# Moving the small attention matmuls inside the gate projections of a hybrid attention and expert block

## The chip, the cores and the metric

The kernel runs on one core of a Trainium2 chip. The time is the device time of one execution in microseconds (us). The engines are named as in the profile: PE is TensorE (matmul), PEld its weight loads, DVE is VectorE, ACT is ScalarE, POOL is GpSimd, SP is SyncE, which here only issues transfers. "L917" is line 917 of the kernel. A row-half is one of the two groups of 64 rows of the array: operands in partitions 0 to 63 use one, those in 64 to 127 the other.

## The reference

256 tokens of width 1024, all in f32, one layer. Shortened:

```python
h = rms_norm(x, norm1_g)
q, k, v, qi, ki, wi, pool_in, gate_a, gate_p = split(h @ w_in)
#    512 128 128 256 64  4   512      1024    1024 columns
q, k = rope(rms_norm(q)), rope(rms_norm(k))        # 8 query heads, 2 key heads of 64
qi, ki = partial_rope(qi), partial_rope(layer_norm(ki))
score = sum_over_heads(relu(qi @ ki.T) * wi)       # 4 index heads
sel = top_k(where(admissible, score, -inf), 64)    # per query
attn = softmax(q @ k[sel].T * scale) @ v[sel]
pooled = per_group_linear(trailing_mean(pool_in) - pool_in) * pool_scale
merged = sigmoid(gate_a) * (attn @ w_a) + sigmoid(gate_p) * (pooled @ w_b)
x = x + merged @ w_out
h2 = rms_norm(x, norm2_g)
x = x + moe(h2)   # router, best 4 of 32 experts, gate_up 1024 x 2048, clamped SwiGLU, down 1024 x 1024
```

## The kernel before

The 256 tokens are two row blocks b of 128. The normalised input is held transposed as hT. The projection with w_in is cut into eight groups of columns (`groups`, L208): 512 with K, V and QI, 68 with KI and the index weights, 512 of Q, 512 of pooling input, then two of 512 for each gate. `projection(j)` (L907) computes group j for both row blocks: two halves of the contraction, each one unit of weights, two row blocks and four steps k of 128 rows, so 16 products, each of which appears as two MATMUL records. Its results lie in one of three pairs of PSUM banks. ScalarE takes them out (`job` L394, `gate_job` L401).

All small matmuls (transposes, scores, mixing) write one of two further banks, `TB[j % 2]`, in a fixed order of numbered jobs TJ_... (L229). `t_job(j)` (L881) waits until job j - 2 has been read; each job is read by one named engine in program order (`tcopy` on ScalarE L408 and on VectorE L668, score readers L654, the pooling L678).

TensorE's program is written out by hand and runs in its order. Before the change it reads: projections 0 to 3; the turns of K, QI and KI and the index scores (L969 to L985, four jobs L0 and L1); projection 4; the turns of Q; projection 5; the attention scores (L993 to L1004, S0 for block 0 and S1 for block 1); projection 6; the turns of the probabilities; projection 7; the mixing with the pooling bands (L1021 to L1023), the attention output (L1032), the per-group map (L1041); the two branch products with w_a, then those with w_b (`branch`, L929, one call per row block); the turn of merged block 0 (L1059); then the product with w_out (L1103 on, with the second turn and the router inside it) and the experts.

VectorE prepares K, KI, QI and Q (L584 to L621), does the top 64 selection (L623 to L643, eight rounds of MAX8 and MATCH_REPLACE8 for each row block), masks the scores while reading them out of the banks (L654), finds the maxima, and scales the probabilities (L665, L666). ScalarE does Exp (L439). Later VectorE multiplies the gates in (`gated`, L683) and adds the branches (L697).

SP issues the weight transfers in one queue. The 24 units of the first part (`pre_unit`, L257) go into twelve half slots. Ten slots of 2 MB then serve the experts: eight for gate and up weights (`gu_slot`, L85), two for down weights. Several hold attention data first, so that each has its own condition for its first load (L282 to L298): slot 0 after projection 6, slot 1 after projection 7, slots 6 and 7 after the attention output, slots 2 and 8 after the branch with w_a, slots 3 and 9 after that with w_b, slots 4 and 5 after w_out. From then on a slot is refilled when its expert is done with it, in the order of `gates_a`, `gates_b`, `downs_a`, `downs_b`. The experts go in 16 pairs with 64 tokens each.

Of the kernel before, what the change touches and what calls it, by code (L numbers as in the profile page):

```python
# [5 lines left out]
P = 128  # L6
# [56 lines left out]
def block_kernel(nc, x_d, pos_d, w_in, w_a, w_b, w_out, mix_d, router_d, w_gu, w_dn, b_dn,  # L63
# [6 lines left out]
    with ctx:  # L70
# [17 lines left out]
        kvqi_t, q_t, pool_t, kqT_t = (slot[6][:, 1024 * j:1024 * j + 1024] for j in range(4))  # L88
        ptb, rt_t = slot[7][:, 0:3072], slot[7][:, 3072:4096]
        qT_t, attnT_t = slot[8][:, 0:1024], slot[8][:, 1024:2048]  # L90
        kdup_t, kidup_t, kiT_t = slot[8][:, 2048:2560], slot[8][:, 2560:2816], slot[8][:, 2816:3072]
        mixw_t, work_t = slot[8][:, 3072:3584], slot[8][:, 3584:4096]
        rel, pooledT_t = slot[9][:, 0:1024], slot[9][:, 1024:2048]
        bands_t, kiwi_t = slot[9][:, 2048:3584], slot[9][:, 3584:3720]
# [31 lines left out]
        kvqi, kiwi = v3(kvqi_t[:, :], NB), v3(kiwi_t[:, :], NB)  # L126
# [14 lines left out]
        mixedT, pooledT = v3(rel, GROUPS), v3(pooledT_t, GROUPS)  # L141
# [82 lines left out]
        def dn_src(e, j):  # L224
# [15 lines left out]
        LAST_OF_BRANCH = {17: 2 * (BJ_WA + NB), 19: 2 * (BJ_WB + NB), 23: 2 * (BJ_WO + NB)}  # L240
# [4 lines left out]
        def _(sp):  # L245
# [44 lines left out]
            sp.wait_ge(job_ready, 2 * (BJ_WA + NB))  # L290
# [3 lines left out]
            sp.wait_ge(job_ready, 2 * (BJ_WB + NB))  # L294
# [78 lines left out]
        def _(act):  # L373
# [43 lines left out]
            job(0, kvqi)  # L417
            job(1, kiwi)
# [28 lines left out]
            for j in range(2):  # L447
                tcopy(TJ_MIX + j, mixedT[:, 2 * j:2 * j + 2, :])
# [60 lines left out]
        def _(dve):  # L509
# [162 lines left out]
            tcopy(TJ_P0 + 1, PT[0][:, 0, 4:8, :])  # L672
            tcopy(TJ_P1 + 1, PT[1][:, 0, 4:8, :])
            tcopy(TJ_P1 + 3, PT[1][:, 1, 4:8, :])

            for j in range(2):
# [3 lines left out]
                                ALU.mult).then_inc(t_read[(TJ_POOL + j) % 2], 1)  # L680
            dve.wait_ge(job_read, 16)
# [193 lines left out]
        def _(pe):  # L875
# [31 lines left out]
            def projection(j, between=None):  # L907
# [61 lines left out]
            pe.wait_ge(roped, 1)  # L969
            transposes(TJ_K, [kdup[:, b, kv, :] for b in range(NB) for kv in range(KV)])  # L970
            pe.wait_ge(roped, 3)
            transposes(TJ_QI, [kvqi[:, b, 256 + P * g:256 + P * g + P] for b in range(NB) for g in range(2)])
            transposes(TJ_KI, [kidup[:, b, :] for b in range(NB)])

            short_read(pe, TJ_KI + 1)
            for b in range(NB):
                nk = P * (b + 1)
                for par in range(2):
                    dst = t_job((TJ_L0, TJ_L1)[b] + par)
                    for i in range(2):  # L980
                        h = 2 * i + par
                        r = 64 * (h % 2)
                        ins = MM(dst[:, i * nk:i * nk + nk], qiT[r:r + 64, h // 2, b * P:b * P + P], kiT_t[r:r + 64, 0:nk],
                                 start=True, stop=True)
                    ins.then_inc(t_ready, 1)  # L985
            projection(4)
            pe.wait_ge(roped, 4)
            for b in range(NB):
                transposes(TJ_Q + b, [qq[:, b, P * g:P * g + P] for g in range(4)])
            projection(5)  # L990

            short_read(pe, TJ_Q + 2)
            for b in range(NB):  # L993
                nk = P * (b + 1)
                per = BANK // nk
                for g in range(HEADS // per):
                    dst = t_job((TJ_S0 if b == 0 else TJ_S1) + g)
                    h0 = 4 * (g // 2) + g % 2 if b == 1 else g
                    for i in range(per):
                        h = h0 + 2 * i  # L1000
                        r = 64 * (h % 2)
                        ins = MM(dst[:, i * nk:i * nk + nk], qT[r:r + 64, h // 2, b * P:b * P + P], kT[r:r + 64, h // 4, 0:nk],
# [336 lines left out]
```

## Time and profile before

| | us |
|---|---|
| median of three timed runs | 1127.81 (1127.17 to 1128.42) |
| profiled execution | 1124.1 |
| its span, first to last instruction | 1122.3 |
| PE busy | 1051.0 (94%) |
| DVE busy | 290.4 (26%) |
| ACT busy | 118.0 (11%) |
| transfers, mean | 383 GB/s over the span |

The page divides the span into 40 slices of 28 us; the GB/s row is what the transfer engines moved in each. A busy PE is not PE at its peak: matmuls overlap, and the distance from one start to the next is the cost. The profiled execution is one run; its time is 3.7 us below the median of the timed ones.

### The profile page before, as it was taken

To read this page: it belongs to the slowest core of one execution; us is meant where nothing else is said; L and a number is where in the kernel's file an instruction comes from. 1 tells how busy PE (TensorE), PEld (TensorE's weight loads), DVE (VectorE), ACT (ScalarE), POOL (GpSimd) and SP (SyncE) were. 2 spreads that over 40 slices of the span, in tenths; PEclk is the share of its full clock that TensorE was granted. 3 is DMA by queue.
4 is the path that set the end of the run, shared out by engine and by line. 5 is a ranking of instruction groups with operands and counts; after the bars stand their busy time and mean duration, and the time that the engine had idled before them with its cause. 6 is when DMAs were issued, how large, how long until landed. Compare 5 with 4: busy or idle time off the path is not lost.

```text
span 1122.3 us, 11997 instructions
## 1 busy us (share of the span) xinstructions
PE 1051.0 (94%) x4830; PEld 439.1 (39%) x4830; DVE 290.4 (26%) x592; ACT 118.0 (11%) x210; POOL 7.7 (1%) x16
## 2 busy tenths in 40 slices
PE   7999999999999999999999989898989899999988
PEld 4444545543434343434343424242424243333332
DVE  2654032332222222221212121221212212212221
ACT  3124101201000000000000000000000000000001
POOL 2000000000000000000000000000000000000000
PEclk9999999999999999999999999999999999999999
DMA  9932573899999999999999999999999999999995
GB/s 335 392 130 84 216 279 117 336 385 430 428 427 428 429 425 427 422 429 429 428 428 427 430 429 429 429 428 429 427 430 429 429 428 428 430 426 430 429 429 220
DMA packets 40256, 430.32 MB, mean 383 GB/s; under 512 B 5024, under 2 KB 5152, under 8 KB 15536
## 3 DMA queue, kind: packets, MB, share of 16 engines
q1 hardware_dynamic: 39280, 428.11, 91.4%
q0 software_dynamic: 672, 1.91, 0.5%
q8 instruction: 11, 0.18, 0.1%
q10 hardware_dynamic: 288, 0.08, 0.0%
q14 instruction: 5, 0.04, 0.0%
HBM read 429.03 MB, written 1.05 MB: 383 GB/s over the span
## 4 chain that ended last, share of the span: by engine, by line
PE 73%; DMA 22%; DVE 2%; issue 1%; ACT 0%; SPq 0%; DVEq 0%
PE bank L1194 28%; DMA slot<-w_gate_up_dram 18%; PE bank L1219 14%; PE bank L917 9%; PE bank L1139 5%; PE bank L1168 5%; DMA slot<-w_down_dram 4%; PE bank L941 4%; PE bank L1208 2%; DVE x L838 2%; PE bank L1117 1%; PE bank L892 1%; PE bank L1179 1%; DMA consts<-consts_dram 0%; PE bank L1235 0%
## 5 line engine op out<-in xcount | busy, mean ns | idle before, releaser
L1194 PE MATMUL bank<-slot,scr 128*64 128x512 f32 x2048 | 458.8, 596 | 20.5 <-DMA slot<-w_gate_up_dram 20.4
L1194 PEld LDWEIGHTS bank<-slot,scr 128*64 128x64 f32 x2048 | 142.3, 137 | 305.9 <-issue 268.6
L1219 PE MATMUL bank<-slot,scr 128*64 128x512 f32 x1008 | 229.1, 596 | 11.1 <-DMA slot<-w_down_dram 10.4
L813 DVE COPY scr<-bank 128x512 f32<-128x512 f32 x32 | 22.1, 691 | 456.6 <-PE bank L1194 456.6
L1219 PEld LDWEIGHTS bank<-slot,scr 128*64 128x64 f32 x1008 | 68.6, 137 | 144.9 <-issue 120.0
L917 PE MATMUL bank<-slot,scr 128*128 128x512 f32 (+1 forms) x256 | 103.3, 563 | 0.8 <-DVE scr L531 0.8
L1168 PE MATMUL bank<-scr 64*128 64x512 f32 x240 | 59.6, 613 | 22.0 <-DVE x L838 22.0
L838 DVE TENSOR_TENSOR x<-bank,x 128x512 f32<-128x512 f32 x64 | 41.4, 686 | 105.3 <-PE bank L1168 103.1
L819 DVE TENSOR_TENSOR scr<-bank,bgu 128x512 f32<-128x512 f32 x64 | 41.2, 686 | 104.9 <-PE bank L1208 104.9
L917 PEld LDWEIGHTS bank<-slot,scr 128*128 128x128 f32 x256 | 46.5, 194 | 53.7 <-issue 52.5
L1139 PEld LDWEIGHTS bank<-scr,xn 128*128 128x128 f32 x480 | 57.7, 196 | 12.2 <-issue 12.2
L1139 PE MATMUL bank<-scr,xn 128*128 128x128 f32 x480 | 60.5, 285 | 0.0
L473 ACT ACTIVATE scr<-bank 128x512 f32<-128x512 f32 x32 | 19.1, 597 | 383.7 <-PE bank L1194 383.7
L1168 PEld LDWEIGHTS bank<-scr 64*128 64x128 f32 x240 | 22.0, 186 | 59.4 <-DVE x L838 34.0
L1208 PEld LDWEIGHTS bank<-consts,scr 128*128 128x128 f32 x256 | 33.3, 210 | 26.9 <-issue 26.9
L1208 PE MATMUL bank<-consts,scr 128*128 128x128 f32 x256 | 39.3, 296 | 0.9 <-ACT scr L473 0.9
L477 ACT ACTIVATE scr<-scr 128x512 f32<-128x512 f32 x32 | 20.2, 631 | 183.2 <-DVE scr L823 183.2
L485 ACT ACTIVATE scr<-bank 128x512 f32<-128x512 f32 x16 | 9.6, 597 | 208.2 <-PE bank L1179 208.2
L941 PE MATMUL bank<-slot 128*128 128x512 f32 x64 | 27.6, 592 | 0.0
L481 ACT ACTIVATE scr<-bank 128x512 f32<-128x512 f32 x31 | 18.5, 597 | 45.4 <-PE bank L1219 45.4
L827 DVE SCALAR_TENSOR_TENSOR scr<-scr 128x512 f32<-128x512 f32 x32 | 22.2, 693 | 3.3
L831 DVE TENSOR_TENSOR scr<-scr 128x512 f32<-128x512 f32 x32 | 22.2, 692 | 1.1
(184 smaller groups left out, 389.1 us busy)
## 6 DMA issues: line engine op xcount, KB each, us to landing
slot<-w_gate_up_dram SPq DMA_DIRECT2D x128, 2048.0 KB, 29.2
slot<-w_down_dram SPq DMA_DIRECT2D x63, 2048.0 KB, 20.9
slot<-w_in_dram SPq DMA_DIRECT2D x14, 1024.0 KB, 15.5
slot<-w_out_dram SPq DMA_DIRECT2D x4, 1024.0 KB, 4.9
slot<-w_branch_attn_dram SPq DMA_DIRECT2D x2, 1024.0 KB, 13.9
slot<-w_branch_pool_dram SPq DMA_DIRECT2D x2, 1024.0 KB, 8.5
slot<-w_down_dram SPq DMA_DIRECT2D x2, 1024.0 KB, 7.2
x<-x_dram SPq DMA_DIRECT2D x2, 512.0 KB, 5.7
```

What stands on the lines that cost most here:

```text
L813: V.tensor_copy(gu_sb[:, 512:1024], GB[1][:, :]).then_inc(gu_copied[1], 1)
L819: V.tensor_tensor(gu1[:, 4 * h:4 * h + 4, :, :], v4(TU[h][:, :], 4, 2), bias.unsqueeze(3).to_broadcast([P, 4, 2, T]), ALU.add).then_inc(re ...
L827: V.scalar_tensor_tensor(out=up1, in0=up1, scalar=1.0, in1=gu1[:, :, 0, :], op0=ALU.add, op1=ALU.mult).then_inc(prod_ready, 1)
L831: V.tensor_tensor(actT[e], up1, sg, ALU.mult).then_inc(act_ready, 1)
L838: V.tensor_tensor(x[:, b, 512 * h:512 * h + 512], XY[h][:, :], x[:, b, 512 * h:512 * h + 512], ALU.add).then_inc(read[f"Y{j}"], 1)
L917: ins = MM(bank[PAIR_BANKS[j % 3][b]][:, 0:n], hT[:, kc, b * P:b * P + P], w[:, k, :], start=kc == 0, stop=kc == KC - 1)
L941: ins = MM(bank[PAIR_BANKS[j % 3][h]][:, :], lhs[:, k, b * P:b * P + P], w[:, k % 2, 512 * h:512 * h + 512], start=k == 0, stop=k == nk - 1)
L1139: ins = MM(XY[h][:, k * P:k * P + P], xn[:, b, c0:c0 + 2 * P - 1:2], selb[:, b * P:b * P + P], start=b == 0, stop=b == NB - 1)
L1168: ins = MM(XY[h][:, :], selgT[T * h:T * h + T, SEQ * e + b * P:SEQ * e + b * P + P], dsb[T * h:T * h + T, 512 * e:512 * e + 512], start=e ...
L1194: ins = MM(GB[h][T * g:T * g + T, :], xgT[:, k, T * e:T * e + T], gu_slot[s][:, c0:c0 + 512], start=k == 0, stop=k == KC - 1)
L1208: ins = nc.tensor.transpose(TU[h][:, k * P:k * P + P], gu_sb[:, c0:c0 + 4 * P - 3:4], ident)
L1219: ins = MM(DB[T * h:T * h + T, :], actT[e][:, c, :], v3(dn_slot[j][:, :], 4)[:, k, 512 * h:512 * h + 512], start=c == 0, stop=c == KC - 1)
```

## The change

- **Narrow columns.** The groups of 512 (K, V, QI) and 68 (KI, weights) become two groups of 290 columns in one tile kvx.
- **Inside the projections.** `projection` takes a table `under`: at step 8 * half + 4 * b + k it calls the functions named there ahead of the product. Turns of K, QI, KI and the index scores go into projection 4; the turns of Q and the scores of row block 0 into 5; the scores of block 1 and the mixing into 6; the turns of the probabilities and the per-group map into 7; the attention output into the first branch product; the turn of merged block 0 into the last.
- **Alternating halves.** In the index scores and the attention scores two jobs are opened together, and successive products use row-half 0 and 1 in turn, into the two banks. Before, a job's products all used one half.
- **Pooling branch first.** The w_b branch comes before the w_a branch, in TensorE's, VectorE's and SP's order; w_b is loaded first. VectorE's second turn copy of a block comes straight after its sum.
- **Orders.** The jobs are renumbered. ScalarE's two mix copies come between the two blocks of Exp. VectorE reads the pooling results between the probability copies.
- **Slots.** The attention tiles are laid out anew in slots 6, 8 and 9, and slots 8 and 9 change places in `gu_slot`.

The core of the diff; the tile layout and the functions that only wrap old code (turn_k, turn_qi, turn_ki, index_scores, turn_probs, mix, pooled, attended, take_pooled) are left out. index_scores has the loop order of scores.

```diff
-        gu_slot = [slot[s] for s in (0, 1, 6, 7, 2, 8, 3, 9)]
+        gu_slot = [slot[s] for s in (0, 1, 6, 7, 2, 9, 3, 8)]
...
-        groups = [(C_K, 512), (C_KI, 68), (C_Q, 512), (C_POOL, 512),
+        groups = [(C_K, 290), (C_K + 290, 290), (C_Q, 512), (C_POOL, 512),
                   (C_GA, 512), (C_GA + 512, 512), (C_GP, 512), (C_GP + 512, 512)]
...
-            w, r0 = [(w_a, 16), (w_b, 18), (w_out, 20)][0 if u < 18 else 1 if u < 20 else 2]
+            w, r0 = [(w_b, 16), (w_a, 18), (w_out, 20)][0 if u < 18 else 1 if u < 20 else 2]
...
-            0, 4, 5, 6, 7, 9, 11, 25, 29, 13, 15, 19, 21, 27, 31, ((35, 36), (38, 40)), (37, 41), (39, 42))
-
-        BJ_WA, BJ_WB, BJ_WO = 8, 10, 12
+            0, 4, 5, 6, 7, 9, 11, 19, 23, 13, 15, 21, 25, 29, 31, ((35, 36), (38, 40)), (37, 41), (39, 42))
+
...
-            sp.wait_ge(job_ready, 2 * (BJ_WA + NB))
+            sp.wait_ge(job_ready, 2 * (BJ_WB + NB))
...
-            sp.wait_ge(job_ready, 2 * (BJ_WB + NB))
+            sp.wait_ge(job_ready, 2 * (BJ_WA + NB))
...
-            job(0, kvqi)
-            job(1, kiwi)
+            job(0, kvx[:, :, 0:290])
+            job(1, kvx[:, :, 290:580])
...
+                if b == 0:
+                    for j in range(2):
+                        tcopy(TJ_MIX + j, mixedT[:, 2 * j:2 * j + 2, :])
...
-            for j in range(2):
-                tcopy(TJ_MIX + j, mixedT[:, 2 * j:2 * j + 2, :])
...
+            tcopy(TJ_P0 + 1, PT[0][:, 0, 4:8, :])
+            for j in range(2):
+                take_pooled(j)
+            tcopy(TJ_P1 + 1, PT[1][:, 0, 4:8, :])
+            tcopy(TJ_P1 + 3, PT[1][:, 1, 4:8, :])
...
+                gated(BJ_WB, b, sigp)
+            for b in range(NB):
                 gated(BJ_WA, b, siga)
-
-            for b in range(NB):
-                gated(BJ_WB, b, sigp)
-                dve.wait_ge(job_read, 2 * (BJ_WB + b) + 2)
+                dve.wait_ge(job_read, 2 * (BJ_WA + b) + 2)
                 V.tensor_tensor(siga[:, b, :], siga[:, b, :], sigp[:, b, :], ALU.add).then_inc(merged_ready, 1)
-            for j in (1, 3):
-                tcopy(TJ_M + j, hT[:, 4:8, (j // 2) * P:(j // 2) * P + P])
+                tcopy(TJ_M + 2 * b + 1, hT[:, 4:8, b * P:b * P + P])
...
+            def projection(j, between=None, under={}):
...
+                            for call in under.get(8 * half + 4 * b + k, ()):
+                                call()
...
+            def turn_q(b):
+                pe.wait_ge(roped, 4)
...
+            def scores(b, pair):
+                short_read(pe, TJ_Q + 2)
                 nk = P * (b + 1)
                 per = BANK // nk
+                j = (TJ_S0, TJ_S1)[b] + 2 * pair
+                dst = [t_job(j + par) for par in range(2)]
+                for i in range(per):
+                    for par in range(2):
+                        h = 4 * pair + par + 2 * i
+                        r = 64 * par
+                        ins = MM(dst[par][:, i * nk:i * nk + nk], qT[r:r + 64, h // 2, b * P:b * P + P], kT[r:r + 64, h // 4, 0:nk],
                                  start=True, stop=True)
+                        if i == per - 1:
+                            ins.then_inc(t_ready, 1)
...
+            projection(4, under={2: [turn_k], 4: [turn_qi], 6: [turn_ki], 9: [lambda: index_scores(0)],
+                                 12: [lambda: index_scores(1)]})
+            projection(5, under={4: [lambda: turn_q(0)], 6: [lambda: turn_q(1)], 13: [lambda: scores(0, 0)]})
+            projection(6, under={1: [lambda: scores(1, 0)], 4: [lambda: scores(1, 1)], 6: [lambda: mix(0)],
+                                 8: [lambda: mix(1)]})
+            projection(7, under={1: [lambda: turn_probs(0, 0, 0)], 3: [lambda: turn_probs(0, 0, 1)],
+                                 5: [lambda: pooled(0)], 7: [lambda: pooled(1)],
+                                 9: [lambda: turn_probs(1, 0, 0)], 11: [lambda: turn_probs(1, 0, 1)],
+                                 13: [lambda: turn_probs(1, 1, 0)], 15: [lambda: turn_probs(1, 1, 1)]})
             short_read(pe, TJ_POOL + 2)
-            for b in range(NB):
-                branch(b, BJ_WB, 18, 4, pooledT)
+            branch(0, BJ_WB, 16, 4, pooledT, ((2, lambda: attended(0)), (3, lambda: attended(1))))
+            branch(1, BJ_WB, 16, 4, pooledT)
+            short_read(pe, TJ_O + 2)
+            branch(0, BJ_WA, 18, 4, attnT)
...
-            turn_merged(0)
+            branch(1, BJ_WA, 18, 4, attnT, ((2, lambda: turn_merged(0)),))
```

## Rows read from the trace of the kernel before

**Rows 1.** The page's part 2, 40 slices of the span, DMA share and GB/s.
```profile
DMA  9932573899999999999999999999999999999995
GB/s 335 392 130 84 216 279 117 336 385 430 428 427 428 429 425 427 422 429 429 428 428 427 430 429 429 429 428 429 427 430 429 429 428 428 430 426 430 429 429 220
```

**Rows 2.** The chain that ended last, in order of time: start us, us, what.
```profile
1067.52 26.57 DMA slot<-w_down_dram
```

**Rows 3.** Waits: engine, line, waited for: us in total, times, longest.
```profile
SPq L255 <- PE bank L1117: 30.1, 1, 30.1
...
DVE slot L654 <- PE bank L1002: 14.5, 1, 14.5
```

**Rows 4.** Timeline of SP: start us, us, what; x8 counts merged issues.
```profile
209.71 37.51 SPq L266 DMA_DIRECT2D slot<-w_gate_up_dram  x8
```

**Rows 5.** Timeline of TensorE, 55 to 213 us, columns as above, idle time before in brackets.
```profile
55.29 1.04 PE L892 MATMUL bank<-consts,slot 128*128 128x128 f32 x8
...
61.09 14.65 PE L917 MATMUL bank<-slot,scr 128*128 128x512 f32 x32
...
76.46 13.90 PE L917 MATMUL bank<-slot,scr 128*128 128x512 f32 x32
90.29 1.71 PE L1002 MATMUL bank<-slot 64*128 64x128 f32 x16
...
94.96 1.73 PE L1002 MATMUL bank<-slot 64*128 64x256 f32 x8 [0.93 <-DVE xn L654]
96.61 14.00 PE L917 MATMUL bank<-slot,scr 128*128 128x512 f32 x32
110.45 1.04 PE L892 MATMUL bank<-consts,slot 128*128 128x128 f32 x8
...
114.31 13.90 PE L917 MATMUL bank<-slot,scr 128*128 128x512 f32 x32
128.05 0.39 PE L1021 MATMUL bank<-slot 128*128 128x128 f32 x2
...
130.82 2.86 PE L1032 MATMUL bank<-slot 128*64 128x256 f32 x24
133.61 1.99 PE L1041 MATMUL bank<-slot 128*128 128x256 f32 x8
135.44 27.63 PE L941 MATMUL bank<-slot 128*128 128x512 f32 x64
162.91 1.04 PE L892 MATMUL bank<-consts,scr 128*128 128x128 f32 x8
165.72 7.13 PE L941 MATMUL bank<-slot,scr 128*128 128x512 f32 x16 [1.77 <-DVE scr L670]
172.69 1.04 PE L892 MATMUL bank<-consts,scr 128*128 128x128 f32 x8
173.56 7.03 PE L941 MATMUL bank<-slot,scr 128*128 128x512 f32 x16
...
206.03 7.09 PE L1194 MATMUL bank<-slot,scr 128*64 128x512 f32 x32 [0.19 <-issue]
```

**Rows 6.** TensorE's groups by shape: line, shapes, count, busy us, mean ns, idle before.
```profile
L917 PE MATMUL bank<-slot,scr 128*128 128x68 f32 x32 | 3.7, 273 | 0.0
```

**Rows 7.** Timeline of TensorE among the experts.
```profile
283.76 1.99 PE L1168 MATMUL bank<-scr 64*128 64x512 f32 x8 [1.47 <-DVE x L838]
285.68 1.51 PE L1194 MATMUL bank<-slot,scr 128*64 128x512 f32 x6
```

**Rows 8.** One stretch: length, busy us of PE, PEld, DVE, ACT, POOL, PEclk, DMA, GB/s.
```profile
60.00:61.00 1.00, 1.00 (x5) 0.35 (x2) 0.86 (x4) 0.19 (x1) 0.00 (x0) 0.50 0.12 49
```

**Rows 9.** Timeline of VectorE: top-k begins and ends, last scaling of probabilities.
```profile
59.13 0.29 DVE L626 TENSOR_SCALAR slot<-slot 128x128 f32<-128x128 f32 x1 [6.98 <-ACT slot L415]
...
76.79 0.29 DVE L643 TENSOR_SCALAR slot<-slot 128x256 f32<-128x256 f32 x1
...
104.28 2.29 DVE L666 TENSOR_TENSOR xn<-xn,small 128x2048 f32<-128x2048 f32 x1
```

More of the change, by code:

```diff
@@ L125, in block_kernel @@
         siga, sigp = v3(siga_t[:, :], NB), v3(sigp_t[:, :], NB)
-        kvqi, kiwi = v3(kvqi_t[:, :], NB), v3(kiwi_t[:, :], NB)
+        kvx = v3(kvx_t, NB)
+        kvqi, kiwi = kvx[:, :, 0:512], kvx[:, :, 512:580]
         qq, pool = v3(q_t[:, :], NB), v3(pool_t[:, :], NB)
@@ L670, in tcopy, with take_pooled @@
                 V.tensor_copy(dst, v3(TB[j % 2][:, :], 4)).then_inc(t_read[j % 2], 1)
[L672 to L676, printed above, removed]
+            def take_pooled(j):
                 dve.wait_ge(t_ready, TJ_POOL + j + 1)
@@ L905, in free_banks @@
                     pe.wait_ge(job_read, 2 * (j - 2))
-            def projection(j, between=None):
+            def projection(j, between=None, under={}):
                 free_banks(j)
@@ L967, in _, with turn_k @@
                 projection(j)
[L969 to L975, printed above, removed]
-            for b in range(NB):
-                nk = P * (b + 1)
[L978 to L983, printed above, removed]
+            def turn_k():
+                pe.wait_ge(roped, 1)
+                transposes(TJ_K, [kdup[:, b, kv, :] for b in range(NB) for kv in range(KV)])
@@ new lines, in turn_qi, with turn_ki, index_scores @@
+            def turn_qi():
+                pe.wait_ge(roped, 3)
+                transposes(TJ_QI, [kvqi[:, b, 256 + P * g:256 + P * g + P] for b in range(NB) for g in range(2)])
+            def turn_ki():
+                transposes(TJ_KI, [kidup[:, b, :] for b in range(NB)])
+            def index_scores(b):
+                short_read(pe, TJ_KI + 1)
+                nk = P * (b + 1)
+                j = (TJ_L0, TJ_L1)[b]
+                dst = [t_job(j + par) for par in range(2)]
+                for i in range(2):
+                    for par in range(2):
+                        r = 64 * par
+                        ins = MM(dst[par][:, i * nk:i * nk + nk], qiT[r:r + 64, i, b * P:b * P + P], kiT_t[r:r + 64, 0:nk],
@@ L984, in _ @@
                                  start=True, stop=True)
[L985 to L988, printed above, removed]
+                        if i == 1:
+                            ins.then_inc(t_ready, 1)
+            def turn_q(b):
+                pe.wait_ge(roped, 4)
                 transposes(TJ_Q + b, [qq[:, b, P * g:P * g + P] for g in range(4)])
-            projection(5)
-            short_read(pe, TJ_Q + 2)
@@ L993, in _ @@
-            for b in range(NB):
+            def scores(b, pair):
+                short_read(pe, TJ_Q + 2)
                 nk = P * (b + 1)
                 per = BANK // nk
[L996 to L1002, printed above, removed]
+                j = (TJ_S0, TJ_S1)[b] + 2 * pair
+                dst = [t_job(j + par) for par in range(2)]
+                for i in range(per):
+                    for par in range(2):
+                        h = 4 * pair + par + 2 * i
+                        r = 64 * par
+                        ins = MM(dst[par][:, i * nk:i * nk + nk], qT[r:r + 64, h // 2, b * P:b * P + P], kT[r:r + 64, h // 4, 0:nk],
@@ L1003, in _, with turn_probs @@
                                  start=True, stop=True)
-                    ins.then_inc(t_ready, 1)
-            projection(6)
-            for b in range(NB):
+                        if i == per - 1:
+                            ins.then_inc(t_ready, 1)
+            def turn_probs(b, kb, g):
                 pe.wait_ge(prob_ready, b + 1)
-                for kb in range(b + 1):
-                    for g in range(2):
-                        transposes((TJ_P0 if b == 0 else TJ_P1) + 2 * kb + g,
-                                   [att[b][:, 4 * g + i, kb * P:kb * P + P] for i in range(4)])
@@ L1013, in _, with mix @@
-            projection(7)
-            pe.wait_ge(late_in, 32)
-            pe.wait_ge(job_read, 8)
-            for j in range(2):
+                transposes((TJ_P0, TJ_P1)[b] + 2 * kb + g,
+                           [att[b][:, 4 * g + i, kb * P:kb * P + P] for i in range(4)])
+            def mix(j):
+                pe.wait_ge(late_in, 32)
+                pe.wait_ge(job_read, 8)
                 dst = t_job(TJ_MIX + j)
@@ L1024, in _, with pooled, attended @@
                 ins.then_inc(t_ready, 1)
-            for b in range(NB):
+            def pooled(j):
+                short_read(pe, TJ_MIX + 2)
+                dst = t_job(TJ_POOL + j)
+                for i in range(2):
+                    g = 2 * j + i
+                    ins = MM(dst[:, i * SEQ:(i + 1) * SEQ], mixw[:, g, :], mixedT[:, g, :], start=True, stop=True)
+                ins.then_inc(t_ready, 1)
+            def attended(b):
+                short_read(pe, TJ_P1 + 4)
                 dst = t_job(TJ_O + b)
```

24 lines of the change are left out of this document (8 added, 16 removed).

## The prediction

> **What bounds the kernel now.** I read the page's DMA rows first [rows 1]. Transfers run at about 428 GB/s from the tenth of the 40 slices to the last but one, and far below that in slices 3 to 7, the time of the attention part. The chain that ended last is, late in the run, mostly waiting for weights, up to 1094.1 us [rows 2]: the expert part ends when the weights have come in. SP's queue brings them. It once waited 30.1 us in one piece for TensorE's w_out product at line 1117 [rows 3], because all slots for experts had their first contents and none could be refilled; its second round of gate and up weights starts at 209.71 us [rows 4]. What is then left is 32 experts x 12.58 MB less the 21.0 MB of the ten slots, 381.7 MB; at 428 GB/s that is 892 us and ends at 1101 us, near where the chain's last waits end. So DMA sets the length from 209.71 us on, and TensorE sets when that stretch begins, since the refill follows the first expert matmuls at 206.03 us [rows 5]. Any microsecond that TensorE loses or saves before 206 us should come out at the end one for one.
>
> The TensorE timeline shows the part before 206 us as a string of matmuls with few idle places [rows 5]. I read start-to-start distances there, not durations, because neighbouring matmuls overlap.
>
> **Prices.** One f32 product of 128x128 with 512 columns is two MATMUL records; 32 records take 13.83 us (76.46 to 90.29), 0.432 each. With 256 columns it is 0.216: line 1041's 8 records take 1.83 us less an edge of 0.1. A transpose costs 0.109: 8 take 0.87 us at 172.69, in the middle of a branch product, with no edge [rows 5]. With 68 columns 32 records fill 3.7 us [rows 6], less 0.16 for the tail of the last: 0.11 each, so few columns come no cheaper than a transpose. For 290 columns I take 290/512 of 0.432, 0.245 each; the bounds are 0.216 (the row with 256 columns) and 0.26 (half of 0.432 and 0.044 more, for weights that come as slowly as they did for 68 columns).
>
> Matmuls of 64 rows that alternate between the halves of the array: line 1168's 8 records of 512 columns go from 283.76 to the next work at 285.68 [rows 7], 1.92 us, which is 4 x 0.432 + 0.2. A pair costs what one costs, and entering and leaving such a group costs about 0.1 each. In the scores of before, the 8 records at 94.96 take 1.65 us [rows 5], nearly 8 x 0.216: two products of one half come in a row there and hardly overlap with those of the other.
>
> **The change part by part**, from the first record to the next product, before [rows 5] against after.
>
> 1. Narrow columns, 512 + 68 as 290 + 290: 32 x 0.432 + 32 x 0.11 = 17.3 us become 64 x 0.245 = 15.7: saves 1.7 (bounds 0.7 to 3.5). The bytes are the same 580 columns; after them the queue stands where it stood.
> 2. Turns of K, QI, KI and index scores: 55.29 to 61.09, 5.80 us. After, under projection 4: 10 transposes 1.09, eight records of 128 columns in pairs 4 x 0.11 + 0.2 = 0.64, eight of 256 columns 4 x 0.216 + 0.2 = 1.06. Total 2.8, saves 3.0. The waits for ScalarE's copies lose their price because at least 1.7 us of projection stands between a turn and its user; without that cover they cost what they did.
> 3. Clock: in 60 to 61 us the granted clock was 0.50, the 1.2 GHz level [rows 8], after a stretch with gaps. Part of that is in item 2; the projection behind it took 14.50 us (61.09 to 76.46 less 0.87 of turns) against 13.83. Without gaps I expect the 2.4 GHz level: saves 0.7 (bounds 0 and 0.7).
> 4. Scores: 90.29 to 96.61, 6.32 us. After: 16 records of 128 columns in pairs 8 x 0.11 + 0.2 = 1.1; two groups of eight with 256 columns, 1.06 each. Total 3.2, saves 3.1. If alternating bought nothing it would be 2.6 less in this and item 2.
> 5. Turns of the probabilities: 110.45 to 114.31, 3.86 us for 24 transposes of 0.109 = 2.6: saves 1.2.
> 6. Mixing, attention output, pooling: 128.05 to 135.44, 7.39 us, become 24 x 0.11 = 2.65, then 24 records in pairs with two edges more, 2.79 + 0.2, then 8 x 0.216 = 1.73: 7.4, saves 0.
> 7. The order of the branches moves nothing by itself. But turn_merged(0) now stands inside the last branch product, where 3.4 us of matmuls cover VectorE's gating; 162.91 to 165.72 was 2.81 us with a stall of 1.77, after it is 8 x 0.109 = 0.87: saves 1.9.
>
> Sum 1.7 + 3.0 + 0.7 + 3.1 + 1.2 + 0 + 1.9 = 11.6 us.
>
> A rule speaks against items 2, 4 and 6: the Trainium skill, TensorEngine Tiling (Array Packing), Tiling Modes, says that a change of the tiling mode, and not merely of the tile, drains TensorE. By that rule each 64-row group put between 128-row products pays at both ends, while inserted transposes pay nothing. The trace agrees and has the size, 0.1 us an end.
>
> **What the moved work waits for.** PE's order is the program's, so a turn that waits holds up the rest of its projection. I laid the new order out with the prices above; projection 4 starts at 53.6.
> - The index scores leave TensorE at 63.1 and 66.7, so VectorE's top-k starts at 63.9 where it started at 59.13, lasts the same 17.95 us (59.13 to 77.08) [rows 9] and ends at 81.9. Before, VectorE then waited 14.5 us for the scores [rows 3], so this delay has cover.
> - scores(0,0) run at 82.2 to 83.2. VectorE reads them by 84.8, TensorE needs the banks again at 86.7. scores(1,1) need the banks of (1,0) at 90.3, read at 89.2; mix(0) needs one at 93.0, read at 92.1. These are the thin places, about 1 us each.
> - On ScalarE the two mix copies are now queued ahead of the second block of Exp, whose input is ready at 95.3; mix(1) comes at 97.5, so that block runs 98.2 to 102.1. The probabilities of rows 128 to 255 are ready at 104.7 (before, 106.57 [rows 9]) and TensorE turns them from 114.6: 10 us of slack.
> - On SP the slots are freed by projections 6 and 7, attended(1) and the two branches, by the layout each 5 to 11 us earlier than before, the last by w_out, which moves by the sum. POOL's two loads follow turn_merged and keep their distance to the router.
>
> TensorE then begins w_out at 154.1 (before 165.72) and the experts at 206.0 - 11.6 = 194.4.
>
> The profiled execution took 1124.1 us around a span of 1122.3; the sum is made against that span, 1110.7 after, or 1112.5 with what lies around it. The median of the timed runs, 1127.81, is 3.7 higher, and I take the same saving off it: 1116.2.
>
> **The rivals.**
> - A, feeding too slow: two of the thin places are late by 2 to 3 us and the clock falls once more, 1.3 us (the 0.7 of item 3 and half a microsecond more in the index scores). That takes 4 to 6 off: about 1121. For it: slacks of 1 us. Against: the durations on VectorE and ScalarE are rows, not guesses.
> - B, each inserted group has edges of 0.1, also transposes between products. Of 23 insertions 16 have none in my sum: 32 x 0.1 = 3.2, 1119.4. Against: the turns at 172.69.
> - C, slower than before: the array empties at each end of all 23 insertions. The price of an end lies between nothing and the part of a record beyond its pitch, 0.16, on both sides of the switch, 0.32. At 0.16 it takes 46 x 0.16 = 7.4: 1123.6. From 0.25 it eats the whole saving, at 0.32 it costs 14.7: 1131. The same row speaks against it; for it, that no row shows a group inside a projection.
> - D, nothing arrives at the end, 1127.8: the expert transfers don't begin earlier though TensorE does. The wait of 30.1 us [rows 3] speaks against it.
>
> **How the numbers follow.** Chances: forecast 0.80 (1114 to 1118, from the bounds of items 1 and 3), A 0.09, B 0.05, C slower than before 0.03, D 0.03. The likeliest is 1116.2. The range goes to 1114 below and takes in B and the better half of A above, 1120.5. A difference of less than 0.2% (2.3 us) can't be told from none here. Faster by more 0.94, within 0.03, slower 0.03.
>
> **What would show it.** Right: records of 290 columns 0.245 us apart; no granted clock below 1.00 from 55 to 65 us; TensorE without idle time over 0.3 us from 12 to 154 us; turns 0.109 apart inside projections; w_out's first product at 154, the first expert matmul at 194.4, and the DMA rows as before, shifted. Wrong: TensorE idle at the second scores or the mix; starts spread around each turn; the second round of expert weights still at 209 us.

## The result, and the profile after

| | before | changed |
|---|---|---|
| median of the timed executions, us | 1127.17 (1123.89 to 1128.42, 5) | 1113.79 (1113.02 to 1118.94, 5) |
| ratio | | 0.9887, 95% interval 0.9868 to 0.9906 |
| profiled execution, us | 1124.1 | 1113.79 |
| its span, us | 1122.3 | 1112.0 |
| mean granted clock in it | 0.998 | 0.999 |

A later set gave 1117.13 us for the changed kernel (6 executions) beside 1127.97 for the kernel before (11), ratio 0.9906 (0.9881 to 0.9931). The forecast was 1116.2 with 1114.0 to 1120.5: the first median, 1113.79, lies just below that range's lower end and the second inside; the ratio's interval puts the saving at 10.6 to 14.9 us, around the forecast 11.6. Two errors of opposite sign are behind this closeness: the parts of the sum brought 1.2 us less than forecast, and the median before holds a fall of TensorE's clock that the changed kernel's first median doesn't.

The timeline of TensorE of the changed kernel, in the columns of [rows 5] (projections are L921, transposes L894, index scores L993, attention scores L1013, attention output L1049, branches L945, experts L1214):

```profile
8.19 2.27 PE L921 MATMUL bank<-slot,scr 128*128 128x290 f32 x4 [0.83 <-DVE scr L533]
...
55.74 0.60 PE L894 MATMUL bank<-consts,slot 128*128 128x128 f32 x4
56.18 1.88 PE L921 MATMUL bank<-slot,scr 128*128 128x512 f32 x4
...
62.94 0.72 PE L993 MATMUL bank<-slot 64*128 64x128 f32 x8
63.59 2.84 PE L921 MATMUL bank<-slot,scr 128*128 128x512 f32 x6
66.36 1.13 PE L993 MATMUL bank<-slot 64*128 64x256 f32 x8
67.42 7.13 PE L921 MATMUL bank<-slot,scr 128*128 128x512 f32 x16
74.39 0.60 PE L894 MATMUL bank<-consts,slot 128*128 128x128 f32 x4
...
83.09 1.16 PE L1013 MATMUL bank<-slot 64*128 64x128 f32 x16
84.18 3.70 PE L921 MATMUL bank<-slot,scr 128*128 128x512 f32 x8
87.81 1.13 PE L1013 MATMUL bank<-slot 64*128 64x256 f32 x8
...
98.93 7.89 PE L921 MATMUL bank<-slot,scr 128*128 128x512 f32 x18
...
123.89 3.60 PE L945 MATMUL bank<-slot 128*128 128x512 f32 x8
127.42 1.08 PE L1049 MATMUL bank<-slot 128*64 128x256 f32 x8
128.43 1.98 PE L945 MATMUL bank<-slot 128*128 128x512 f32 x4
...
151.26 1.04 PE L894 MATMUL bank<-consts,scr 128*128 128x128 f32 x8
152.14 3.60 PE L945 MATMUL bank<-slot 128*128 128x512 f32 x8
155.57 7.03 PE L945 MATMUL bank<-slot,scr 128*128 128x512 f32 x16
...
195.73 7.09 PE L1214 MATMUL bank<-slot,scr 128*64 128x512 f32 x32
```

Behind the row at 8.19 us no row carries idle time in brackets until 192.35, where [rows 5] had 0.93 and 1.77 us among the rows shown. w_out begins at 155.57 (165.72 before) and the experts at 195.73 (206.03 before): 10.3 us earlier. The page's GB/s row, in the place of [rows 1], and SP's row that answers to [rows 4]:

```profile
GB/s 332 392 179 91 173 370 157 339 385 428 427 428 428 430 423 429 421 431 428 428 429 428 428 429 428 428 428 429 428 429 428 428 429 428 428 428 429 428 428 217
```
```profile
199.41 37.48 SPq L267 DMA_DIRECT2D slot<-w_gate_up_dram  x8
```

The refill of the expert slots starts 10.3 us earlier (209.71 before), and the rate behind it is the same 428 GB/s. From the first expert matmul to the end it is 1122.3 - 206.0 = 916.3 us before and 1112.0 - 195.7 = 916.3 us after. So in these two traces TensorE's gain arrives at the end one for one. Over the nine profiles of this document without the long clock fall that is described below, this last stretch takes 916.1 to 917.2 us, so that a span by itself tells what a part is worth only to about a microsecond.

### The profile page after: what moved, and what is told of

It reads as the page before. It is cut to its first block, busy times and chain, and to the rows that moved or that the text cites. A ratio compares the mean times of both kernels' runs of the same rounds, so it can differ in the third digit from the quotient of the medians.

```text
span 1112.0 us, 12017 instructions
## 1 busy us (share of the span) xinstructions
PE 1045.5 (94%) x4830; PEld 438.2 (39%) x4830; DVE 290.7 (26%) x592; ACT 118.2 (11%) x210; POOL 7.7 (1%) x16
## 4 chain that ended last, share of the span: by engine, by line
PE 74%; DMA 23%; DVE 2%; issue 1%; SPq 0%; ACT 0%; DVEq 0%
PE bank L1214 28%; DMA slot<-w_gate_up_dram 18%; PE bank L1239 14%; PE bank L921 9%; PE bank L1159 5%; PE bank L1188 5%; DMA slot<-w_down_dram 4%; PE bank L945 4%; PE bank L1228 2%; DVE x L840 2%; PE bank L1137 1%; PE bank L894 1%; PE bank L1199 1%; DMA consts<-consts_dram 0%; PE bank L1255 0%
## 5 line engine op out<-in xcount | busy, mean ns | idle before, releaser
L1214 PE MATMUL bank<-slot,scr 128*64 128x512 f32 x2048 | 458.8, 596 | 20.5 <-DMA slot<-w_gate_up_dram 20.4
L1214 PEld LDWEIGHTS bank<-slot,scr 128*64 128x64 f32 x2048 | 142.3, 137 | 305.8 <-issue 268.5
L1239 PE MATMUL bank<-slot,scr 128*64 128x512 f32 x1008 | 229.1, 596 | 11.2 <-DMA slot<-w_down_dram 10.4
L921 PE MATMUL bank<-slot,scr 128*128 128x512 f32 (+1 forms) x256 | 103.5, 553 | 0.8 <-DVE scr L533 0.8
L921 PEld LDWEIGHTS bank<-slot,scr 128*128 128x128 f32 x256 | 47.4, 192 | 42.3 <-issue 37.2
L945 PE MATMUL bank<-slot 128*128 128x512 f32 x64 | 28.3, 595 | 0.0
```

Source lines behind the costliest of these rows:

```text
L945: ins = MM(bank[PAIR_BANKS[j % 3][h]][:, :], lhs[:, k, b * P:b * P + P], w[:, k % 2, 512 * h:512 * h + 512], start=k == 0, stop=k == nk - 1)
L1214: ins = MM(GB[h][T * g:T * g + T, :], xgT[:, k, T * e:T * e + T], gu_slot[s][:, c0:c0 + 512], start=k == 0, stop=k == KC - 1)
L1239: ins = MM(DB[T * h:T * h + T, :], actT[e][:, c, :], v3(dn_slot[j][:, :], 4)[:, k, 512 * h:512 * h + 512], start=c == 0, stop=c == KC - 1)
```

## The experiments

All are compared with the changed kernel. "Experts at" is the start of the first expert matmul, and a figure in parentheses behind a median is the number of executions. Two distances of the TensorE timeline serve as measures: from the first record of projection 0 to the turn of K (47.55 us in the changed kernel), called *start*, and from the turn of K to w_out (155.57 - 55.74 = 99.83 us), called *middle*. They leave out where the first matmul happens to begin.

**Columns back to 512 and 68.**

```diff
-        groups = [(C_K, 290), (C_K + 290, 290), (C_Q, 512), (C_POOL, 512),
+        groups = [(C_K, 512), (C_KI, 68), (C_Q, 512), (C_POOL, 512),
...
-            job(0, kvx[:, :, 0:290])
-            job(1, kvx[:, :, 290:580])
+            job(0, kvx[:, :, 0:512])
+            job(1, kvx[:, :, 512:580])
```


> The changed kernel with the narrow columns put back to groups of 512 and 68; all else as changed. Theory (each part counts by its own TensorE time, and that time reaches the end one for one): projections 0 and 1 take 17.3 us again in place of 15.6, the first expert matmul comes 1.5 to 1.7 us later than the changed kernel's 195.7 us, near 197.3, and the span grows from 1112.0 to about 1113.6. Rival (few columns cost nothing extra, the saving lies elsewhere): experts and span within 0.3 us of the changed kernel.

Measured: experts at 197.63, span 1114.3, median 1116.51 (4). The middle is 99.83, unchanged, the start 49.89, 2.3 longer. Not all of that is the columns: among profiles with the same columns the start differs by over 1 us, 47.5 to 48.7 in the nine with 290 columns and 49.1 to 50.4 in the five with 512 and 68 (two steps of 0.86 added where projection 4 begins behind the turn of K). The start is longer where TensorE's granted clock rises later: it does so at 10.9 to 13.9 us, and until then a record of 512 columns takes 0.853 us instead of 0.429. Of profiles in which it rises at the same time within 0.3 us, those with 512 and 68 columns have a start longer by 1.6 to 1.8: 49.10 against 47.55 (rise at 11.2 and 11.5), 49.47 against 47.80 (11.7), 49.89 against 48.20 (12.7 and 12.5), 50.40 against 48.63 (13.9). So the columns are worth about 1.7 us, at the upper end of the theory, and the rest of the 2.3 is the clock's later rise (12.7 against 11.5 us).

**Products of a score job in a row, both banks opened first.** In `scores` and `index_scores`:

```diff
-                for i in range(per):
-                    for par in range(2):
+                for par in range(2):
+                    for i in range(per):
```


> The changed kernel with the products of a score job issued job by job, so that successive matmuls use the same half of the array; two banks are still opened together. Theory: groups of eight records with 256 columns take 1.65 us from first to next instead of about 1.07, the 16 records of 128 columns 1.5 to 1.9 instead of 1.09, the eight of 128 columns up to 0.4 more; in all 2.3 to 3.2 us later experts, near 198.4, and a span near 1114.7. Rival (the saving at the scores came from the vanished waits alone): groups unchanged, span within 0.3 us of 1112.0.

Measured: experts at 196.03, span 1113.0, median 1114.56 (4); middle 100.41, only 0.57 longer. Its TensorE timeline:

```profile
66.09 1.14 PE L993 MATMUL bank<-slot 64*128 64x256 f32 x8
67.17 7.13 PE L921 MATMUL bank<-slot,scr 128*128 128x512 f32 x16
...
82.83 1.71 PE L1013 MATMUL bank<-slot 64*128 64x128 f32 x16
84.47 3.70 PE L921 MATMUL bank<-slot,scr 128*128 128x512 f32 x8
```

The group of eight lasts 1.08 us although four records of one half come before four of the other: they run in pairs all the same. Only the group of sixteen, eight of each half, grows, from 1.09 to 1.64. The theory falls: alternating is worth 0.57 us, not 2.6. The rival is right on the groups of eight and wrong on the group of sixteen.

**The same with each job's wait just before its own products.** Shown against the last run:

```diff
-                dst = [t_job(j + par) for par in range(2)]
+                dst = {}
                 for par in range(2):
+                    dst[par] = t_job(j + par)
                     for i in range(per):
```


> The changed kernel with the products of a score job issued job by job and each job waiting for its own bank just before its products, as in the kernel before, but still inside the projections. Theory (two halves overlap when the second job's bank is free, whichever order the products have; before, VectorE's read of the second bank held them apart): groups of eight records take 1.07 us as in the run with two banks opened together, since both banks have long been read. Rival (the wait between the jobs itself keeps them apart): 1.65 us each, three groups, 1.8 us later in all.

Measured: experts at 196.26, span 1113.2; middle 100.41, as in the last run, and groups of 1.07 (88.33 to 89.40 us). So the wait instruction doesn't separate the halves either. What did, in the kernel before, stands in VectorE's timeline of that kernel:

```profile
94.21 1.29 DVE L654 SCALAR_TENSOR_TENSOR xn<-bank,slot 128x512 f32<-128x512 f32 x2
```

These two reads end at 95.50. The group that starts at 94.96 in [rows 5] needs for its second job the bank that the second of them reads, and its records of the other half follow from 95.56 on. In the group that starts at 92.31 it is the same: VectorE's read of the second bank ends at 92.85, and the other half follows from 92.90 on. So what kept the halves apart was a bank not yet read, and the move into the projection, not the loop order, removed that wait.

**All calls ahead of their projection.** The table `under` is kept, but `projection` makes its calls before its first product.

```diff
             def projection(j, between=None, under={}):
+                for at in sorted(under):
+                    for call in under[at]:
+                        call()
...
-                            for call in under.get(8 * half + 4 * b + k, ()):
-                                call()
```


> The changed kernel with all calls of the table under made ahead of their projection and none inside it; order of jobs, halves, columns and branches as changed. Theory (the projection's products are cover for reads by the other engines): TensorE waits again between turn and user, about 0.4 to 0.6 us at ten to twelve places and over 1 us at the second and third score groups, and the granted clock falls below 1.00 at least once for another microsecond or so; experts 5 to 8 us later, 201 to 204, span 1117 to 1120. Rival (edges inside projections eat what the cover gives): experts less than 2 us later.

Measured: experts at 205.60, span 1121.9, median 1120.87 (10); ratio to the kernel before 0.9952 (0.9936 to 0.9967). From projection 4's first record or turn to w_out it is 110.38 us against 101.55 in the changed kernel (99.83 and the two steps ahead of the turn of K). Its TensorE timeline around projection 6, and the stretch behind (columns of [rows 8]):

```profile
90.94 1.13 PE L1014 MATMUL bank<-slot 64*128 64x256 f32 x8
93.61 1.13 PE L1014 MATMUL bank<-slot 64*128 64x256 f32 x8 [1.54 <-DVE xn L656]
95.59 0.52 PE L1030 MATMUL bank<-slot 128*128 128x128 f32 x2 [0.84 <-DVE xn L656]
...
99.97 13.90 PE L922 MATMUL bank<-slot,scr 128*128 128x512 f32 x32
```
```profile
96.00:98.00 2.00, 2.00 (x11) 2.00 (x11) 1.97 (x2) 0.24 (x2) 0.00 (x0) 0.50 0.00 0
```

TensorE waits 1.54 and 0.84 us for VectorE, then mixes at the 1.2 GHz level: 4.38 us for what takes 2.68 in the changed kernel. That is 8.8 us in all, 1.7 of them clock. The experts come 9.9 us later, more than the 5 to 8 expected, since the start is 1.1 longer as well (the clock rises at 13.9 us). The profiled execution, at 1123.78 us, is one of the two slow ones of ten; the other eight lie at 1120.4 to 1121.0, and the median is 7.1 later than the changed kernel's first. The theory holds in kind, with waits at nine places where it had ten to twelve; this is the largest part of the change. Moving the calls inside is worth about 7 us with the row halves, columns and branch order already in place.

**Turn of merged block 0 behind the last branch product.**

```diff
-            branch(1, BJ_WA, 18, 4, attnT, ((2, lambda: turn_merged(0)),))
+            branch(1, BJ_WA, 18, 4, attnT)
+            turn_merged(0)
```


> The changed kernel with the turn of merged block 0 behind the last branch product instead of inside it. Theory: a stall of about 1.8 us behind the turn (ScalarE's and VectorE's copies and, ahead, the sum) returns; VectorE has finished the sum of block 0 before, so the stall may be only the two copies, 0.7 to 1.8 us. Experts 0.7 to 1.9 us later. Rival (branch order alone removed it): within 0.3 us.

Measured: middle 100.78, 0.94 longer, with an idle gap of 0.78 us before w_out; experts at 197.41, span 1117.0, median 1115.82 (4). The theory's 0.7 to 1.9 holds at its lower part: VectorE's sum is done before the turn, so only the copies behind it are bare, where [rows 5] had 1.77. The other microsecond of that wait is VectorE's order. In the kernel before VectorE copied the turn at 164.98, behind the gating and the sum of block 1 (from 162.25 on); here it copies at 156.41, ahead of them. The span is 5 us longer, not 1: TensorE's granted clock was 0.50 for some seven microseconds in the first pair of experts, and from the first expert matmul to the end it took 919.6 us. This long fall is the subject of the last three runs.

**Inside the projections alone.** The three edits above together: columns, products in a row, turn behind.


> The changed kernel with three parts put back: groups of 512 and 68, products of a score job issued job by job, turn of merged block 0 behind the last branch product. What is left is the moving of turns and scores into the projections (and the branch order). Theory (parts add up): 2.3 us (columns) + 0.55 (halves) + 0.95 (turn) later than the changed kernel, experts near 199.5, span near 1115.8. Rival (parts overlap, one hides another): less than 2.5 us later.

Measured: middle 101.35, 1.52 longer (0.57 + 0.94 = 1.51); start 49.47, 1.9 longer; experts at 198.74, span 1118.7, median 1119.05 (9). The theory holds: the parts add up in the middle to 0.01 us, and the start's 1.9 lies within the spread given above. Against the kernel before, the experts begin 7.3 us earlier (198.74 against 206.03): so much do the moves into the projections bring, together with the order of the branches and of the copies.

**One group instead of two for the attention output.**

```diff
-            branch(0, BJ_WB, 16, 4, pooledT, ((2, lambda: attended(0)), (3, lambda: attended(1))))
+            branch(0, BJ_WB, 16, 4, pooledT, ((2, lambda: attended(0)), (2, lambda: attended(1))))
```


> The changed kernel with both attention outputs at step 2 of the first branch product, so that one group of column-split products stands there instead of two. Theory (each group of another tile shape pays about 0.4 us: 0.1 each on leaving the 128x128 form, on its own first record, on return, and on the first record after): the branch part is 0.4 us shorter, w_out 99.4 us behind the turn of K instead of 99.83. Rival (edges of 0.2 as in the forecast): 0.2 us shorter.

Measured: middle 99.49, 0.35 shorter, nearer to 0.4 than to 0.2. Experts at 196.67, span 1113.1, median 1115.7 (5). The times show no gain: in the profile the clock falls to 0.50 from 193 to 197 us, and from w_out to the experts it takes 41.38 us instead of 40.16.

**The scores of block 0 twice, together and apart.** The first set's products are computed again by the second. `scores` gets two more arguments for this, the banks to write and whether to signal; that part of the edit is left out here.

```diff
-            projection(5, under={4: [lambda: turn_q(0)], 6: [lambda: turn_q(1)], 13: [lambda: scores(0, 0)]})
+            projection(5, under={4: [lambda: turn_q(0)], 6: [lambda: turn_q(1)],
+                                 13: [lambda: scores(0, 0, scores(0, 0, None, False))]})
```


> The changed kernel with the 16 records of the scores of row block 0 issued twice, one set right behind the other (the first set's result is overwritten). Theory: 8 pairs of 0.11 more, 0.9 us, in one group: it goes from 1.09 to 1.98 us.

```diff
+                                 10: [lambda: early.append(scores(0, 0, None, False))],
+                                 13: [lambda: scores(0, 0, early[0])]})
```


> The same doubling, but the first set stands three steps earlier in projection 5, a group of its own. Theory: 0.9 us for the products and about 0.4 us for one more group between 128x128 products; projection 5 is 1.3 us longer than the changed kernel's, 0.4 more than with both sets together. Rival (an edge costs 0.1 on each side): 0.2 more than together. Rival (an inserted group is free when its operands are ready): no difference.

Together, TensorE's timeline:

```profile
83.51 2.06 PE L1013 MATMUL bank<-slot 64*128 64x128 f32 x32
85.50 3.70 PE L921 MATMUL bank<-slot,scr 128*128 128x512 f32 x8
```

Apart:

```profile
76.75 3.60 PE L921 MATMUL bank<-slot,scr 128*128 128x512 f32 x8
80.28 1.16 PE L1013 MATMUL bank<-slot 64*128 64x128 f32 x16
81.37 2.84 PE L921 MATMUL bank<-slot,scr 128*128 128x512 f32 x6
84.14 1.16 PE L1013 MATMUL bank<-slot 64*128 64x128 f32 x16
85.23 3.70 PE L921 MATMUL bank<-slot,scr 128*128 128x512 f32 x8
```

The group together lasts 1.99 us, as expected (1.98). The middle is 100.73 together (0.89 longer) and 101.12 apart (1.29): one more group costs 0.40 us. The places: eight records of 512 columns take 3.53 from 76.75 to 80.28 where 8 x 0.429 is 3.43 (0.1 on leaving); the six from 81.37 to 84.14 take 2.77 where 6 x 0.429 is 2.57 (0.1 on the first after the group, 0.1 on leaving again); the group itself takes 1.09 where 8 x 0.11 is 0.88 (0.2 inside, on its first record and on return). Experts at 197.05 and 196.78, spans 1116.9 and 1112.9: the 4 us between the spans, against the order of the work, are the same long fall, which the first of the two profiles has (919.9 us behind the first expert matmul) and the second hasn't (916.1).

**The kernel before, profiled a second and a third time.**


> The kernel before, looked at once more, to see where TensorE's granted clock falls in it. Theory: a fall from 59 to 63 us, which costs 1.3 us, and in more than half of the executions a second fall of about 7 us at 0.50 in the first pair of experts, near 232 to 240 us, as three of the profiles of changed kernels show it at 221 to 230; mean clock 0.995 and about 1127.5 us with it, 0.998 and 1124 without. Rival: the second fall lies at another place with gaps (the scores, the turns of the probabilities, the turn of merged).

> The kernel before, a third look; the same expectation as for the second look.

The second: 1124.58 us, span 1122.8, mean clock 1.00, and no fall between the rise in the first 14 us and the end, not even the one expected at 59 to 63 us. The third: 1129.6 us, span 1126.1, mean clock 0.995. Its stretches from 61 to 62 us and in the first expert pair, and TensorE's timeline there:

```profile
61.00:62.00 1.00, 1.00 (x3) 0.50 (x2) 0.86 (x5) 0.63 (x2) 0.00 (x0) 0.50 0.05 20
...
233.00:235.00 2.00, 2.00 (x5) 0.53 (x6) 0.69 (x1) 0.00 (x0) 0.00 (x0) 0.50 1.07 459
```
```profile
228.33 5.08 PE L1154 MATMUL bank<-scr 32*128 32x512 f32 x8
233.34 5.87 PE L1194 MATMUL bank<-slot,scr 128*64 128x512 f32 x16
```

In this execution the theory holds: a short fall where the turns and index scores stand with gaps, and a long one from 231 to 238 us. The long one begins during the bias product, the eight records of L1154 (L1174 in the changed kernel) that use 32 rows of the array. The rival's places, the scores, the turns of the probabilities and the turn of merged, showed none. The short fall is in two of the three profiles of this kernel.

**The changed kernel once more.**


> The changed kernel once more, for its spread beside the kernel before on one chip. Theory (10.3 us of TensorE's time ahead of the experts, and the rest of the difference of the medians is clock): most executions near 1113.5 at a mean clock of 0.998 or more, a few near 1117 to 1119 at 0.996 or 0.997; a difference to executions of the kernel before with a clock of 0.998 or more of about 10.5 us, and a difference of the medians of 11 to 14 us.

Six executions: 1117.51, 1117.36, 1117.31 and 1116.96 at 0.997 or 0.998, 1113.06 and 1113.43 at 0.999. The profiled one, 1117.51, has the long fall and not the short one; its middle is 99.83 to the hundredth, its experts begin at 195.84, and it takes 919.9 us from there:

```profile
222.00:224.00 2.00, 2.00 (x6) 0.69 (x8) 0.69 (x1) 0.00 (x0) 0.00 (x0) 0.50 1.07 459
...
226.00:236.00 10.00, 10.00 (x58) 5.58 (x55) 0.00 (x0) 0.60 (x1) 0.00 (x0) 0.93 0.70 249
```

The last of these stretches in the first profile of the changed kernel, without the fall:

```profile
226.00:236.00 10.00, 10.00 (x62) 5.69 (x60) 0.00 (x0) 0.03 (x1) 0.00 (x0) 1.00 0.96 385
```

The transfers drop from 385 to 249 GB/s, since the slots of the first expert pair come free later. "A few near 1117" was too low, here it is four of six. Without the long fall the difference is as expected: 1113.06 and 1113.43 beside five of the kernel before at 1123.3 to 1125.1, about 10.5. The difference of the medians, 10.8, is just below the theory's 11 to 14.

## Why the prediction was right, and what was off in it

Each item of the sum, from the timelines of the two kernels. Two boundaries need a step back: projection 4 starts two steps before the turn of K, 55.74 - 4 x 0.429 = 54.02; projection 5 four steps before the turn of Q, 74.39 - 8 x 0.429 = 70.96; projection 7 starts 16 of 18 records behind 98.93, at 105.80.

| item | before | after | saved | forecast |
|---|---|---|---|---|
| 1 start up to projection 4 | 47.38 | 45.83 | 1.55 | 1.7 |
| 2, 3 turns, index scores, projection 4 | 20.30 | 16.94 | 3.36 | 3.7 |
| 4 Q, scores, projections 5 and 6, less 2.68 of mixing | 34.86 | 32.16 | 2.70 | 3.1 |
| 5 probabilities, projection 7, less 1.72 of the map | 17.60 | 16.37 | 1.23 | 1.2 |
| 6 mixing, attention output, map | 7.39 | 7.73 | -0.34 | 0 |
| 7 turn of merged | 2.81 | 0.88 | 1.93 | 1.9 |
| sum | | | 10.4 | 11.6 |

With the first projection 0.28 us later than before this is the 10.15 us by which w_out begins earlier.

- **What bounds, and the one for one.** Right for the part ahead of the experts: 916.3 us behind the first expert matmul in both kernels, and the same 428 GB/s. "DMA sets the length from 209.71 us on" was too early. From 236 to 246 us the transfers of the kernel before run at 362 GB/s in its first profile and at 242 in its third, which has the long fall, and that fall, some 7 us at half the clock, arrives at the end with 3.0 to 3.6 us. So TensorE's time still counts in the first pair, when its matmuls free the slots. TensorE itself first waits for expert weights at 593 us in the changed kernel.
- **The price of a group of another shape** was the mis-sized term: 0.2, read from its start to the next record, where 0.40 is right, since the product ahead of it and the first one behind it are each 0.1 longer as well. Five groups of 64 rows and two column-split ones stand between 128x128 products after the change, so items 2, 4 and 6 saved 0.3 to 0.4 less each. Rival B had the right kind of term but put it on the transposes, which cost nothing: 55.74 to 56.18 is 0.44 for four.
- **Item 4's reason was wrong.** Its sum was near, but the price of "one half in a row" was taken from a group whose second bank VectorE was still reading. Alternating bought 0.57 us and not 2.6. The bound given for "alternating buys nothing" was thus not one of alternating at all.
- **Item 1**: records of 290 columns come 0.244 apart (0.245 forecast), and the start is 1.6 to 1.8 us shorter at an equal rise of the clock (1.7 forecast). Right.
- **Item 7** was right in size, 1.93, but only half for its reason. The place inside the branch product is worth 0.94; the rest is that VectorE now copies the turn ahead of block 1's gating and sum, which the forecast didn't price.
- **The thin places held.** VectorE read the first scores from 84.36 and TensorE never waited for it; rival A did not occur. The run with all calls ahead shows what the cover is worth, 7 us and a clock fall.
- **Item 3, the clock, was right in kind and 0.4 short.** The short fall costs 1.6 us, by the first two profiles of the kernel before: from the turn of K to w_out 110.42 with it and 108.82 without. The sum had 0.7 for it and half a microsecond inside item 2. Since one of three profiles of that kernel has no short fall, this part of the saving isn't there in every execution.
- **The same saving off the median was the wrong step.** The 3.7 us between the profiled execution of before and the median were taken as fixed. What the runs show in its place is the long fall: 3.0 us in the third profile of the kernel before (919.35 from the first expert matmul to the end against 916.3), 3.6 in the changed kernel's second profile. It comes or stays away in executions of both kernels, and the profile that the forecast was made from didn't have it. Of the changed kernel's eleven timed executions five lie at 1117 to 1119 and six at 1113.0 to 1114.6; of the kernel before's 37 executions timed beside the experiments, 23 lie above 1126 and 14 at 1123.1 to 1125.1. Without that fall the two kernels are 10 to 11 us apart, as the traces say; medians differ by 10.8 to 13.4, by which of the two groups each median falls into. That the forecast, 1116.2, came within 2.4 us of the first median and 0.9 of the second is luck: it was taken off a median that held the long fall, and it lies between the changed kernel's two groups, near 1113 and near 1117.

Why the long fall comes in some executions and not in others was not tested. By times and mean clocks it was in none of the ten executions with all calls ahead, none of the four each with columns or halves put back, and in four of six of the changed kernel's second set. In all five profiles that have it, it begins 2.7 to 3.2 us behind the first record of the bias product. What differs between the profiles is the distance from the clock's first rise to that product. Nine profiles have it near 206 us: 205.0 to 205.4 in the three with the fall, 205.7 to 206.7 in the six without. In the other five it is 208.5 and 215.8 with the fall, and 213.2, 213.3 and 216.3 without. In the two profiles of the changed kernel the product starts at 217.3 and 217.4 us, behind the same work and the same idle time, but the clock first rises at 11.5 us in the one without the fall and at 12.4 in the one with it. In these traces, then, the coming of the fall goes with when the clock first rises. No run moved or changed the bias product, so that it causes the fall is an inference. One profile, that with the attention output in one group, had another short fall at 193 to 197 us, just ahead of the experts, for which no run gives a reason.

## What to carry to other kernels

Small matmuls with a reader on another engine are best put inside a long product that needs nothing of them: 1.7 to 3.6 us of cover between two of them was enough, and this was worth 7 of the 10 us here. A group of another tile shape cost 0.4 us between full products, transposes of the full shape nothing, so put the former together where their operands allow it and spread the latter. Before a price is read from a group of matmuls, look whether all its banks were free; and before a saving is taken off a median, look at the clocks of the executions behind that median.

## What the runs showed of the hardware that was not expected

- Records of the two row halves run in pairs without alternating in the program, when four of one half stand ahead of four of the other (1.08 us for eight of 256 columns, 1.07 alternating). With eight ahead of eight the second half begins 0.55 us behind the first, between the fifth and the sixth record (1.64 against 1.09 us).
- The rule quoted in the forecast, from the Trainium skill's TensorEngine Tiling (Array Packing), Tiling Modes, agrees with the doubled scores: a change of the tile shape costs 0.40 us for going there and back.
- The granted clock falls to 0.50 in some executions without idle time of TensorE near it: in the changed kernel's second profile it was 0.50 from 222 to 224 us in a stretch busy throughout, while the same stretch of its first profile had 1.00. It began at 220.6 us during eight records that use 32 rows of the array, about 8 us behind the last idle time (0.9 us), and cost 3.6 us. The short fall of the kernel before, in contrast, follows a stretch with gaps. By the Trainium skill, TensorE: Matmul & The Clock Gate, Part 1, the gate goes by how busy TensorE has been recently. The short fall agrees with that; the long one, in a stretch that the profile shows busy throughout, neither bears it out nor refutes it, since no run tested what counts as busy.
